# Half of a projection moved in among the first attention blocks, in a two-layer decoder trunk on one NeuronCore

## The reference, cut to what matters

```python
def shared_kv(x, g_kv, w_kv, g_k):
    kv = rms_norm(x, g_kv) @ w_kv
    k, v = jnp.split(kv, 2, axis=-1)          # 4 key heads of 64 each
    k = rms_norm(k.reshape(b, s, N_KV_HEADS, HEAD_DIM), g_k)
    return to_band(k), to_band(v)             # each block sees itself and the one before

def swa_sink_attention(x, k_band, v_band, g_norm, w_q, g_q, sinks, w_o):
    q = rms_norm((rms_norm(x, g_norm) @ w_q).reshape(b, s, N_Q_HEADS, HEAD_DIM), g_q)
    logits = einsum(q, k_band) * HEAD_DIM ** -0.5 + bias   # blocks of 128 tokens x 256 keys
    m = max(max(logits), sink); p = exp(logits - m)
    p = p / (sum(p) + exp(sink - m))
    return einsum(p, v_band) @ w_o
```

## Time and profile before

| | us |
|---|---|
| median of 3 runs | 1968.12 (1965.95 to 1970.1) |
| the profiled execution | 1967.59 |
| its span in the trace | 1965.8 |
| PE busy | 1924.4 (98%) |
| DVE, ACT, POOL busy | 1495.8, 932.3, 449.2 |

### The profile page before, as it was taken

The page is one execution under the profiler, slowest core; times in us unless marked ns, Lnnn a source line. Parts: engine busy times, 40 slices in busy tenths (PEclk is TensorE's granted clock), DMA queues, the critical chain, the costliest instruction groups (busy, mean ns, idle before and its releaser), DMA issues.

```text
span 1965.8 us, 27856 instructions
## 1 busy us (share of the span) xinstructions
PE 1924.4 (98%) x9704; PEld 1633.8 (83%) x9704; DVE 1495.8 (76%) x2179; ACT 932.3 (47%) x1628; POOL 449.2 (23%) x321
## 2 busy tenths in 40 slices
PE   7999999999999999999999799999999999999999
PEld 7988878878888888888999688877788888888887
DVE  6356758888888876888744688899887888876875
ACT  5233535544444444444412788766444444444443
POOL 0000001333332310020210445442332333301010
PEclk9999999999999999999999899999999999999999
DMA  4111232122212249871111000030221222169681
GB/s 176 44 44 43 86 129 107 65 86 85 85 69 101 86 159 304 248 187 18 44 44 65 22 12 12 22 119 33 90 93 75 85 85 85 65 243 309 186 176 65
DMA packets 62822, 199.01 MB, mean 101 GB/s; under 512 B 5008, under 2 KB 5136, under 8 KB 55568
## 3 DMA queue, kind: packets, MB, share of 16 engines
q1 hardware_dynamic: 48080, 163.29, 23.5%
q0 software_dynamic: 14656, 34.61, 8.1%
HBM read 162.22 MB, written 35.65 MB: 101 GB/s over the span
## 4 chain that ended last, share of the span: by engine, by line
PE 88%; DVE 6%; ACT 3%; issue 1%; DMA 1%; POOL 0%; SPq 0%; DVEq 0%; ACTq 0%
PE banks L2183 28%; PE banks L2185 28%; PE banks L2184 28%; PE banks L2539 1%; ACT lg L1325 1%; DVE xT L1732 1%; DVE xT L1739 1%; PE banks L2513 1%; DMA b<-c_scratch 1%; PE banks L2514 1%; PE banks L2501 1%; DVE fw_lo L1690 0%; PE banks L2302 0%; PE banks L2301 0%; DVE xT L1748 0%
## 5 line engine op out<-in xcount | busy, mean ns | idle before, releaser
L2183 PE MATMUL banks<-t_hi,fw_hi 128*128 128x512 f32 x1248 | 489.1, 392 | 8.8 <-ACT xT L1056 4.2
L2185 PE MATMUL banks<-t_hi,fw_lo 128*128 128x512 f32 x1248 | 486.9, 390 | 0.0
L2184 PE MATMUL banks<-t_lo,fw_hi 128*128 128x512 f32 x1216 | 474.3, 390 | 0.0
L2183 PEld LDWEIGHTS banks<-t_hi,fw_hi 128*128 128x128 f32 x1248 | 234.9, 188 | 61.8 <-ACT xT L1056 5.0
L2185 PEld LDWEIGHTS banks<-t_hi,fw_lo 128*128 128x128 f32 x1248 | 235.0, 188 | 49.2
L2184 PEld LDWEIGHTS banks<-t_lo,fw_hi 128*128 128x128 f32 x1216 | 229.1, 188 | 47.9 <-issue 0.5
L675 POOL TENSOR_TENSOR nrm<-raw 128x512 f32<-128x512 f32 x40 | 55.7, 1392 | 731.9 <-DVE fw_lo L1690 432.9
L2183 PE MATMUL banks<-fw_hi,fw_hi 128*128 128x512 f32 x544 | 211.8, 389 | 1.3 <-DVE fw_lo L1846 1.3
L2185 PE MATMUL banks<-fw_hi,fw_lo 128*128 128x512 f32 x544 | 211.6, 389 | 0.0
L2184 PE MATMUL banks<-fw_lo,fw_hi 128*128 128x512 f32 x544 | 211.6, 389 | 0.0
L1154 ACT ACTIVATE fw_hi<-b 128x512 fp32r<-128x512 f32 x154 | 97.0, 631 | 227.4 <-PE banks L2185 215.2
(11 more groups left out here) (200 smaller groups left out, 4179.5 us busy)
## 6 DMA issues: line engine op xcount, KB each, us to landing
raw<-in_w_f_in SPq DMA_DIRECT2D x44, 1024.0 KB, 4.9
c_scratch<-xT SPq DMA_DIRECT2D x44, 512.0 KB, 2.6
b<-c_scratch SPq DMA_DIRECT2D x16, 1024.0 KB, 9.4
a_sum<-in_w_f_out POOLq DMA_DIRECT2D x16, 1024.0 KB, 14.6
raw<-in_w_f_out SPq DMA_DIRECT2D x54, 256.0 KB, 10.1
w_raw<-in_w_ao SPq DMA_DIRECT2D x16, 512.0 KB, 3.6
x_scratch<-xT SPq DMA_DIRECT2D x4, 2048.0 KB, 7.8
xT<-x_scratch SPq DMA_DIRECT2D x8, 1024.0 KB, 17.7
```

The source lines that it names most:

```text
L2183: nc.tensor.matmul(out, w_h, m_h, start=start, stop=False, **kw)
L2184: nc.tensor.matmul(out, w_h, m_l, start=False, stop=False, **kw)
L2185: return nc.tensor.matmul(out, w_l, m_h, start=False, stop=stop, **kw)
```

## The change

The projection to v is cut into two token halves. Tiles 0 to 3 are done after the fourth q set, in banks 6 and 7; tiles 4 to 7, in banks 4 and 5, in attention blocks 0 to 3 of group 0, two slots of 12 matmuls in each block between q's transposes and the logits. q's transposes of blocks 0 and 1 go to bank 2, as bank 6 holds v. v is evicted in two halves, in blocks 0 and 4 on DVE; ACT's and POOL's parts of v for group 0 go to blocks 0 and 4 (from 0 and 2).

The keys are transposed within the fourth q set (into banks 4 and 5), and the four q sets are written out instead of looped. The splits of w_o's first pair move: slot 0 on ACT to block 2 and on DVE to block 3, slot 1 on ACT to block 4 and on POOL to block 5. Group 0's biases for group 1 move from block 3 to 5. The 1 MB load waits until block 5, and w_o's second to fourth pairs stand behind it.

So that attention's tiles can be written while half of the tokens is still in use, `h_hi_b`, `h_lo_b`, `o_hi` and `o_lo` become two tiles each, one for a token half; kT_hi, kT_lo, qT and the logits of blocks 0 to 5 (`lg_first`) move into other regions. The tail slots move too, with their waits, and the copy of the second token half waits for the whole of layer 0's last product (it was so for its last three tiles only).

The diff, cut to its core:

```diff
-        h_hi_b = sb("h_hi_b", [P, KT, T], F32R, at)
-        h_lo_b = sb("h_lo_b", [P, KT, T], F32R)
+        h_hi_b = [sb(f"h_hi_b{half}", [P, KT, HALF], F32R, at + 32 * 1024 * half) for half in range(2)]
+        h_lo_b = [sb(f"h_lo_b{half}", [P, KT, HALF], F32R, at + (16 + 32 * half) * 1024) for half in range(2)]
...
+            pairs(w_o, (0, 1))
+            sp.wait_ge(pT_full, LG_FIRST)
             quad(0, w_f_in[QUADS])
-            pairs(w_o, (0, 4))
+            pairs(w_o, (1, 3))
...
-                    if n in (0, 2):
-                        v_lower(j, n // 2)
-                    if j == 0 and n == 2:
+                    if n in ((0, 2) if j else (0, 4)):
+                        v_lower(j, 1 if n else 0)
+                    if j == 0 and n == 5:
                         split(1)
...
-                if half and k >= 5:
+                if half and k == 0:
                     act.wait_ge(prod_full, PROD_F)
...
-                    elif n == TAIL:
-                        act.wait_ge(fw_ready, w2 + 5 * PAIRS + 3 + 1)
+                    elif n < TAIL + 3:
+                        act.wait_ge(fw_ready, w2 + 5 * PAIRS + 4 + n - TAIL + 1)
...
-                    if n in (0, 2):
+                    if j == 0 and n in (0, 4):
+                        act.wait_ge(cols_free[1], 1 + COLS_ALL + n // 4)
+                        v_upper(0, n // 4)
+                    if j and n in (0, 2):
                         v_upper(j, n // 2)
                     if j == 0 and n == 2:
+                        act.wait_ge(cols_half, halves.add())
+                        split(0)
+                    if j == 0 and n == 4:
+                        act.wait_ge(cols_full[1], COLS_ALL + 1)
                         split(1)
...
-                        if n == 3:
+                        if n == (3 if j else 5):
                             biases(j + 1)
...
+            q_columns(1)
+            q_columns(0)
+            act.wait_ge(cols_free[1], 2 + COLS_A)
+            k_twice(0)
+            q_upper(0, 0)
+            q_columns(1)
             act.wait_ge(consts_done, 7)
             biases(0)
-            keys_upper()
-            q_copy(1)
-            act.wait_ge(cols_free[1], 1 + COLS_ALL)
+            act.wait_ge(gain_ready, 1)
+            keys_upper(4)
+            q_columns(0)
+            nc.scalar.preload_act_table(ACT.Exp)
+            q_copy(1, 2)
             q_upper(0, 1)
...
                     if n == TAIL:
-                        dve.wait_ge(c_ready, c0 + 5 * PAIRS + 9)
+                        dve.wait_ge(c_ready, c0 + 5 * PAIRS + 3)
...
+            def values(half):
+
+                n = slice(4 * half, 4 * half + 4)
+                dve.wait_ge(cols_full[1], COLS_ALL + half)
+                nc.vector.tensor_tensor(vv_sb[:, n, :], flat(6 - 2 * half, 2).rearrange("p (n c) -> p n c", c=NKV * HD),
+                                        small[:, 0, n].unsqueeze(2).broadcast_to([P, 4, NKV * HD]),
+                                        ALU.mult).then_inc(cols_free[1], 1)
...
                     nc.vector.tensor_tensor(sink_arg, negm, sinks, ALU.add).then_inc(negm_done, 1)
+                    if j == 0 and n in (0, 4):
+                        values(n // 4)
+                    if j == 0 and n == 3:
+                        split(0)
...
-            split(0)
-            dve.wait_ge(cols_full[1], COLS_ALL)
-            nc.vector.tensor_tensor(vv_sb[:, :, :], flat(4, 4).rearrange("p (n c) -> p n c", c=NKV * HD),
-                                    small[:, 0, 0:NCH].unsqueeze(2).broadcast_to([P, NCH, NKV * HD]),
-                                    ALU.mult).then_inc(cols_free[1], 1)
-            keys_lower()
+            q_columns(1, 0)
+            q_columns(0, 1)
+            q_columns(1, 2)
+            keys_lower(4)
+            q_columns(0, 3)
...
-            def q_body(i):
-                columns(1, h_hi_b, h_lo_b)
-                columns(0, h_hi_b, h_lo_b)
-            loop(0, 2, [(use[0], 2), (use[1], 2), (cols[0], 1), (cols[1], 1)], q_body)
-            columns(1, h_hi_b, h_lo_b)
...
+            def v_slot(half, slot):
+
+                kh, n = slot // 4, 4 * half + slot % 4
+                to = banks[:, 6 - 2 * half + slot % 4 // 2, n % 2 * 256:(n % 2 + 1) * 256]
+                for k in range(4 * kh, 4 * kh + 4):
+                    w = slice(k % 4 * 256, (k % 4 + 1) * 256)
+                    mm = three(to, h_tile(h_hi_b, k, n), h_tile(h_lo_b, k, n), w_hi[:, kh, w], w_lo[:, kh, w],
+                               k == 0 and n % 2 == 0, k == KT - 1, skip_group_check=True)
+                if half and slot == 3:
+                    mm.then_inc(cols_half, 1)
+                elif slot == 7:
+                    mm.then_inc(cols_full[1], 1)
...
+                    if block == 1:
+                        pe.wait_ge(cols_free[1], 1 + COLS_ALL)
                     if more or not last:
-                        q_transpose(2)
+                        q_transpose(2, 2 if block == 0 else 6)
+                    if block < 4:
+                        v_slot(1, 2 * n)
+                        v_slot(1, 2 * n + 1)
+                    if j == 0 and last:
+                        pe.wait_ge(cols_free[1], 2 + COLS_ALL)
                     if j or last:
                         step_out(n, 0)
...
-            keys_transpose()
+            columns(1, h_hi_b, h_lo_b)
+            columns(0, h_hi_b, h_lo_b)
+            columns(1, h_hi_b, h_lo_b)
+            columns(0, h_hi_b, h_lo_b, None, {(0, 4): keys_first})
             pe.wait_ge(cols_free[1], cols[1].now())
-            q_transpose(1)
+            for kh in range(2):
+                pe.wait_ge(w_ready[kh], use[kh].add())
+                for n in range(4):
+                    v_slot(0, 4 * kh + n)
+                    if (kh, n) == (1, 2):
+                        pe.wait_ge(cols_free[0], cols[0].now())
+                        q_transpose(1, 2)
             pe.wait_ge(kT_ready, grp.now())
             logits(0, 1)
```

More of the change, by code:

```diff
@@ L277, in build, with lg_of @@
         slopes = sb("slopes", [P, NKV * QPK], F32)
[L278 to L282, removed]
+        vd_hi = sb("vd_hi", [P, NCH, 2, HD], F32R, at)
         vd_lo = sb("vd_lo", [P, NCH, 2, HD], F32R)
-        qT = sb("qT", [P, QPK, P], F32R)
-        lg = sb("lg", [P, 2, QPK, 2, P], F32)
         pT_hi = sb("pT_hi", [P, 2, 2, QPK * P], F32R)
         pT_lo = sb("pT_lo", [P, 2, 2, QPK * P], F32R)
-        bias_j = [bias_0, sb("bias_1", [P, QPK, 2, P], F32)]
+        o_hi, o_lo = [], []
+        for half in range(2):
+            o_hi.append(sb(f"o_hi_{half}", [P, 2, HALF], F32R))
+            o_lo.append(sb(f"o_lo_{half}", [P, 2, HALF], F32R))
+        lg_later = sb("lg_later", [P, 2, QPK, 2, P], F32)
+        bias_j = [bias_0, sb("bias_1", [P, QPK, 2, P], F32)]
+        kT_hi = sb("kT_hi", [P, T], F32R, nrm_at + 2 * 4 * HB)
+        kT_lo = sb("kT_lo", [P, T], F32R, fw_2_at)
+        qT = sb("qT", [P, QPK, P], F32R, nrm_at)
+        lg_first = sb("lg_first", [P, 2, QPK, 2, P], F32, raw_1_at)
+        def lg_of(block):
+            return lg_first if block < LG_FIRST else lg_later
         banks = ctx.enter_context(nc.psum_tensor("banks", [P, 8, HALF], F32))
@@ L1324, in core @@
                     for h in range(QPK):
[L1325 removed]
+                        nc.scalar.activation(lg_of(block)[:, n % 2, h, b0:2, :], lg_of(block)[:, n % 2, h, b0:2, :], ACT.Exp,
                                              bias=small[:, 6, h:h + 1], scale=-1.0, accum_out=small[:, 7, h:h + 1])
@@ L1950, in kv_lower @@
             def kv_lower(half, k):
-                tok = slice(half * HALF, (half + 1) * HALF)
                 if half == 0 and k == 0:
@@ L2043, in o_lower @@
                     part = slice(e * HD, (e + 1) * HD)
-                    last = nc.vector.tensor_tensor(o_lo[part, :, m * P:(m + 1) * P], o_ps[part, :, e, :],
-                                                   o_hi[part, :, m * P:(m + 1) * P].bitcast(F32), ALU.subtract)
+                    t = slice(m % 4 * P, (m % 4 + 1) * P)
+                    last = nc.vector.tensor_tensor(o_lo[m // 4][part, :, t], o_ps[part, :, e, :],
+                                                   o_hi[m // 4][part, :, t].bitcast(F32), ALU.subtract)
                 last.then_inc(o_ready, 1)
@@ L2263, in out_bank, with pair_out @@
                 outs[b].add()
-            def pair_out(b, slot, d, half, c_hi, c_lo):
-                tok = slice(half * HALF, (half + 1) * HALF)
+            def pair_out(b, slot, d, c_hi, c_lo):
                 out_bank(b, [(w_hi[:, slot, k * 512 + d * P:k * 512 + (d + 1) * P],
                               w_lo[:, slot, k * 512 + d * P:k * 512 + (d + 1) * P],
-                              c_hi[:, k, tok], c_lo[:, k, tok]) for k in range(2)])
-            def pair_outs(slot, c_hi, c_lo):
-                pe.wait_ge(w_ready[slot], use[slot].add())
-                for d in range(4):
-                    for half in range(2):
```

(2 more changed lines are left out.)

106 lines of the change are left out of this document (51 added, 55 removed).

## The result

The changed kernel takes 1957.2 us (median of 6 runs, 1954.6 to 1960.1); the kernel before, timed beside it, 1966.5 us (6 runs, 1965.1 to 1970.1). The ratio is 0.9948, 95% interval 0.9938 to 0.9958, so 8 to 12 us come off. The forecast was 1955.0, 12.6 us off, in a range from 1951.5 to 1961.5. The time is in the range and the sign is right; the forecast itself was some 2 us too low: 1957.2 lies above the band that it gave itself (1953.5 to 1956.5) and at the lower end of that of rival (1), the fall of the clock (1957 to 1959.5). It was also counted from the profiled execution of the kernel before, 1967.6, which lies 1 us above the median of six; as a gain, 12.6 us were forecast and 9.3 measured. The profiled execution took 1959.4 us (span 1957.7), so it gained only 8.2 us on that of before.

A forecast was written before the change was run, and what follows sets the result against it. PE was taken to bound the kernel, except in attention group 0 (blocks 0 to 7), bound by the chain from block to block. 14.2 - 0.9 - 0.7 = 12.6 us off 1967.6 gave 1955.0, range 1951.5 to 1961.5.

The forecast's parts named there:

- rival (1): The clock falls in blocks 4 to 7, losing 2 to 4.5 us, total 1957 to 1959.5; chance 20%.
- Stretch 1: From the fourth q set's end to block 0's logits: 12.8 us instead of 27.0, 14.2 us less.
- The wait for the eviction of the fourth set: Within v's first half: eviction ends 9.7 us after the q set, PE asks at 10.1; no wait, 0.4 us to spare.
- Stretch 2: Block 0's logits to block 4's: v's slots fill PE's waits, 19.9 us instead of 19.0, 0.9 us longer.
- the wait for POOL's q: In blocks 0 to 3, q's transpose may still wait for POOL: between 0 and 1.8 us, taken as 0.8.
- rival (2): v's slots in blocks 0 to 3 aren't hidden but lengthen the chain: 10.6 us more, 1965.6; chance 8%.
- Stretch 3: Block 4's logits to group 1's: ACT's additions make it 27.3 us, 0.7 us longer.
- the prediction's own signs of being wrong: PE idling over 1 us a block beside v's slots, a clock drop, or DVE or POOL in blocks 4 to 6's waits.
- Rival (3): ACT's additions cost nothing and the clock's fall near 1413 goes: 0.7 and some 1.7 us less, 1952.6; chance 9%.
- Rival (4): The clock, down in blocks 4 to 7, stays at 1.2 GHz into groups 1 to 3; 1975 at 40 us; chance 3%.
- The shared port: DVE's split moved into block 3 may meet POOL: 1.25 us more on DVE, 0.9 more in the sum, 1955.9.
- The edits with one answer: Tail slots, later copies of the second token half, delayed loads and unrolled q sets: nothing, or a few covered tenths on DVE.

The follow-up runs named there:

- e_nofill: Changed kernel with each of v's 8 slots in blocks 0 to 3 cut to one matmul of 12 (outputs not the reference's); 1952.0 us, one run.
- e_keys_late: Changed kernel with the keys transposed after v's first half, right ahead of the logits, instead of within the fourth q set; 1960.2 us, ratio 0.9964 to before.
- e_bias: Changed kernel with the next group's biases made in block 1 instead of block 5; 1952.7 us, ratio 0.9921 to the kernel before.
- b_warm: Kernel before with matmuls that nobody reads in the waits of blocks 0 to 3; 1966.9 us, ratio 1.0000.
- r_after: The changed kernel run again, nothing altered; 1956.8 us, ratio 0.9944 to the kernel before.
- e_ahead: Changed kernel with all eight slots of v's second half ahead of block 0 instead of in blocks 0 to 3; 1966.7 us, ratio 0.9997 to before.
- r_before: The kernel before run again, nothing altered; 1970.4 us, one run.
- e_full2: Changed kernel with biases in block 1 and unread matmuls in blocks 5 and 6, ahead of layer 1's ConvFFN and at two ConvFFN waits; 1952.8 us, ratio 0.9926.

## Why the prediction was right, step by step

- **Stretch 1.** Forecast 14.2 us less, measured 14.21 (49.94 less 35.73). The windows show PE full to the logits, as the sum of 0.88 + 11.5 + 0.44 had it. The keys are the part whose cover was tested: 2.70 us in place when they lose it. The wait for the eviction of the fourth set, with 0.4 us to spare in the sum, didn't appear.
- **Stretch 2.** Forecast 0.9 longer, measured 0.71. Of the sum, 19.1 us of PE work was right (19.46 busy); the wait for POOL's q, guessed at 0.8 between 0 and 1.8, was 0.2. That the chain ends before PE's work here, which decides against rival (2), is what e_nofill measures: 17.1 us of chain against 19.7 of PE. The margin is 2.6 us in four blocks.
- **Stretch 3.** The forecast of the intervals was 4.9, 6.05, 6.2, 10.2, in sum 27.3. Measured where the clock stayed up (e_keys_late): 4.86, 6.02, 6.15, 10.19, in sum 27.22. In the changed kernel the first three are 4.86, 6.02 and 6.15 too, and the last is 11.69, since it is run in part at 1.2 GHz. So without the fall the three terms give 14.21 - 0.71 - 0.65 = 12.85 us, against 12.6 forecast. The reading that ACT sets blocks 4 to 7 was tested by e_bias: the interval from block 6's logits to block 7's falls from 6.15 to 4.96 when the biases leave it. That is 1.2 of 1.7 us, so ACT isn't the whole chain, and PE waits 0.5 us for DVE's low part of the probabilities in block 4 (L2570 in the waits of the result).
- **The step that was mis-sized** is rival (1), the clock in blocks 4 to 7, which the sum had at nothing. It was given 20% and 2 to 4.5 us, and happened in both profiled executions of the changed kernel at 1.5. So two of the prediction's own signs of being wrong showed: the clock dropped, and DVE is named in the waits of blocks 4 to 6. The time is right because the terms of the chain are, and because the fall was short. Its case against, that the clock stayed at 1.00 at 61% busy, was one execution's luck: in the kernel before too it was lowered there the second time (1115.9). The price was too high, since it laid 14 us of half clock over these blocks and the fall lasted 3.4, which can lose 1.7 us of PE's work; nearly all of that was lost here, and 1.4 in b_warm. With it the sum is 14.2 - 0.7 - 2.15 = 11.4 us to the start of group 1, and 11.3 is what the first pair of profiles shows there (12.2 the second, whose kernel before had the fall too). The prediction took it that what is saved there comes off the end. It didn't hold in single executions, nor on the mean (11.8 us there, 10.4 at the end): of the 11.3 us, 8.1 were left at the end, since the falls near 1306 and 1409 cost 3.2 us more than in that profile of before; of the 12.2, 12.6.
- **Rival (3)** had one thing right: the lowered clock near 1413 can cost nothing or 1.6 us, but it shifts from run to run, not with the change alone. That it goes was wrong; in the profiles it went only when both waits were filled. That ACT's additions cost nothing was wrong too: stretch 3 is 0.65 us longer at full clock. **Rival (4)** had no part: in the changed kernel each lowered stretch was over after 3.4 or 6.8 us. The range's upper end isn't the sum that it names, which is 1959.5 + 0.9 + 1.7 = 1962.1.
- **The shared port.** The split that moved into block 3 took 1.22 us, as in the earlier trace rows where POOL was idle, because POOL had just ended, at 1092.00. Rows of DVE and of POOL in the changed kernel:

```profile
1092.37 1.22 DVE L1437 TENSOR_TENSOR w_lo<-w_raw,w_hi 128x1024 fp32r<-128x1024 f32 x1
```
```profile
1090.10 1.90 POOL L802 TENSOR_TENSOR lg_first<-lg_first,small 128x1024 f32<-128x1024 f32 x1
```

  They missed each other by 0.37 us. What a meeting costs, the kernel before shows elsewhere. The split of 2.47 us at 970.79 did meet POOL, whose instruction was under way until 972.19:

```profile
970.29 1.90 POOL L738 TENSOR_TENSOR w_raw<-w_raw,par 128x1024 f32<-128x1024 f32 x1 [19.16 <-DMA w_raw<-in_w_q]
```

  Of its 45 splits of this form, the 41 that ran beside no POOL instruction took 1.20 to 1.23 us; the four that met one took 2.07 to 2.47, each 1.08 us more than the time beside it. So the split ends as if it had waited for POOL to end. The 1.25 us of the prediction is one case; right behind the start of a POOL instruction of 1.90 us it would be 1.90 + 1.08 - 1.22, some 1.8 us (an estimate from these rows). What a meeting in block 3 would do to the total was not tested.
- **The edits with one answer** cost nothing that shows. The copies of the second token half start 1.4 us later, as worked out, and DVE behind them at 945.63 instead of 945.50:

```profile
944.96 4.28 ACT L1036 ACTIVATE h_hi_b<-xT 128x512 fp32r<-128x512 f32 x8 [4.38 <-DVE xT L1898]
...
945.63 8.50 DVE L1972 TENSOR_TENSOR h_lo_b<-xT,h_hi_b 128x512 fp32r<-128x512 f32 x8
```

What stays open: the medians of e_bias and r_after differ by 4.1 us, of which 2.5 are found in place. Part of the rest may be falls: the profiled execution of e_bias, with 6.8 us of half clock near 1304 and a mean clock of 0.997, is its slowest (1957.1 us); the other four have 0.998 and 1951.7 to 1953.1 us, and r_after's five have 0.996 to 0.998. Where their falls lay isn't on record, so this isn't shown, and the two kernels ran on different chips.

## What to carry to other kernels

Where a chain across engines sets a stretch and another stretch is one engine's alone, cut the second into slots and put them ahead of the waits of the first: here 11.5 us of matmuls cost 2.6 (e_ahead and e_nofill against the changed kernel). The Trainium skill, Perfetto Trace Analysis, section Optimization Strategy, advises such interleaving of regimes; this case bears it out with that number. Before a slot is placed, lay the chain's length beside the filled engine's work block by block. Then move side work of the engine that sets the chain (the biases) into the blocks that no longer wait for it, and don't read a low granted clock beside waits as a loss before unread matmuls have shown what it is worth.

## What the runs showed of the hardware

A half clock is cheap where a chain sets the pace: 13.6 us of it in blocks 0 to 3 cost 1.6 us (19.01 against 17.39), and e_ahead ran the same blocks in 17.14 with 3.4 us of it. Ahead of a wait 3.4 us of it cost nothing (the 200 matmuls around the two waits of layer 0: 49.83 us in the kernel before, 49.86 in e_ahead without a fall), behind the last wait 1.4 to 1.6 us. In the kernels of the table it began within waits of PE of 1.4 to 3.0 us or up to 1.7 us behind their end, but not at each of them: behind the wait of 2.23 us in block 6 the clock stayed at 1.00 in e_keys_late, and behind the wait of 3.0 us at layer 1's ConvFFN it stayed at 1.00 (before), or was at 0.50 for 3.4 us (r_before, r_after) or 6.8 us (after). The Trainium skill, TensorE: Matmul & The Clock Gate, section What's actually happening, says that the chip's look at PE's activity runs free of the kernel, so that the same kernel differs from run to run; the rows agree. With these waits filled by unread matmuls the granted clock was 1.00 from layer 0's ConvFFN to the last matmul (e_full2), and the kernel was no faster than with the biases moved alone.

VectorE's subtraction of two SBUF inputs (128x1024) took 1.20 to 1.23 us alone, and 1.08 us plus the time beside it when a GpSimd instruction was under way (2.47 us with 1.39 us beside it, kernel before).
